# A transformer stack on one core: weights' slots and all later tiles placed 32 bytes further on

## The chip, the cores and the metric

The kernel runs on one core of a Trainium2 chip. The metric is the device time of one execution in microseconds, from the first to the last instruction. Lower is better.

## What is computed

Four layers work on 256 latent tokens and 256 context tokens of width 1024. Each layer has a token mixer of its own kind (grouped-query attention, differential attention, gated linear attention, neighbourhood attention) and then a gated MLP with a width-3 convolution. Every half is followed by a layer norm, and scales and shifts come from a modulation vector.

```python
def conv_ffn(h, w_up, conv_w, conv_b, w_down):
    u = dwconv_centred(h @ w_up, conv_w, conv_b)
    gate, val = jnp.split(u, 2, axis=-1)
    return (jax.nn.silu(gate) * val) @ w_down
...
for i in range(DEPTH):
    h = x * (1.0 + scale) + shift            # for latents and for context
    x = layer_norm(alpha * x + gate * mixer(h), ln1_g[i], ln1_b[i])
    h = x * (1.0 + scale2) + shift2
    x = layer_norm(alpha * x + gate2 * conv_ffn(h, ...), ln2_g[i], ln2_b[i])
```

In the last layer only the 256 latents go through the output projection and the MLP.

## The kernel before

Activations lie with the feature on the partition and the token in the free dimension: 128 partitions, 8 blocks of features, 512 tokens (columns 0 to 255 context, 256 to 511 latents). Every large projection is done with split numbers. A float32 value x is written as x_hi (rounded to the type fp32r) plus x_lo (the rest). `three` (L1649, the matmul itself on L1652) then issues three matmuls for each block of 128 input features: weights hi by activations hi, weights hi by activations lo, weights lo by activations hi. One of the two operands is stationary (128 columns are loaded into the array, LDWEIGHTS) and the other moves through it (256 or 512 columns). The load for the next matmul runs while the present one moves.

Weights come in slabs of 128 partitions x 1024 float32 (512 KB), by DMAs that the SP queue issues. There are four slots (`SLOTS`). Each has a raw tile `slab_raw`, a rounded one `slab_hi` that ScalarE writes (L571), and a rest `slab_lo` that VectorE writes (L1015). One output tile takes one slab and 24 matmuls. Loads and splits run three slabs ahead (`AHEAD`).

`place` (in `build_program`) hands out positions in a partition one after the other, each rounded up to 64 bytes: first `xn`, then the rounded activations `h_hi` and `h_lo` (16384 bytes each), then the four `slab_raw`, four `slab_hi` and four `slab_lo` (4096 bytes each), then the constants `cst`, the tables, the work tiles of the layer norm and the MLP, and last the tiles of each stage, which share one stretch. The MLP's second product reads `g_hi` and `g_lo`, which lie in that last stretch. `out_z` and `out_gb` of the end lie over `h_hi` and `h_lo`.

The stages of a layer follow each other: projections to q, k, v (`project`, `four_ahead`, and `v_wide` or `v_project`, where the activations are stationary and the slab moves), the mixer, the output projection, the MLP's first product (44 slabs, with `h_hi` and `h_lo` moving), its second product (24 slabs, with `g_hi` and `g_lo` moving). In layers 0 to 2 the MLP's products move 512 columns, in layer 3 they move 256. During the MLP of layers 0 to 2 VectorE also sums the next layer's modulation weights (L1040), and a group of eight short matmuls (L1726) takes these sums up now and then. The layer with gated linear attention also has one small projection whose weights `z_hi` and `z_lo` (64 columns) lie in the last stretch.

Of the kernel before, what the change touches and what calls it, by code (L numbers as in the profile page):

```python
# [47 lines left out]
PARTS_AHEAD = 2  # L48
PART_BUFS = 3
PLANES = 6  # L50
C_HV = C_VAL // C_HEADS
def constants():
    k = np.zeros((P, K_N), np.float32)
    i = np.arange(P)
    k[:, K_ID:K_ID + P] = np.eye(P)
    k[i ^ 32, K_SWAP + i] = 1.0
    k[:, K_ONES:K_ONES + P] = 1.0
    k[:, K_MEAN:K_MEAN + P] = 1.0 / D
    k[:, K_HEAD:K_HEAD + P] = (i[:, None] // HD == i[None, :] // HD)
    t = np.arange(LAT)  # L60
    nf = HD // 4
    inv = (np.float32(1.0) / np.float32(10000.0) ** (np.arange(nf, dtype=np.float32) / np.float32(nf))).astype(np.float32)
    ang = np.concatenate([(t // GRID_W).astype(np.float32)[:, None] * inv,
                          (t % GRID_W).astype(np.float32)[:, None] * inv], -1).astype(np.float32)
    pair = i % 32
    k[:, K_COS:K_COS + LAT] = np.cos(ang).T[pair]
    k[:, K_SIN:K_SIN + LAT] = np.sin(ang).T[pair] * np.where(i % HD < 32, -1.0, 1.0)[:, None]
    k[:, K_EPS], k[:, K_EPS + 1], k[:, K_EPS + 2] = NORM_EPS, LN_EPS, 1.0
    k[[C_RANK, 32 + C_RANK], K_EPS + 3] = 1.0
    for j in range(P // TILE):  # L70
        for r in range(2 * GROUPS):
            k[TILE * j + r, K_SEL + r] = 1.0
    cq = np.arange(GRID_W)
    c0 = np.clip(cq - WIN_C // 2, 0, GRID_W - WIN_C)
    col_in = (cq[None, :] >= c0[:, None]) & (cq[None, :] < c0[:, None] + WIN_C)
    window = np.tile(np.where(col_in, 0.0, -1e30).astype(np.float32)[::-1], (2, 1))
    return k, window
# [126 lines left out]
def build_program(nc, a, layers=DEPTH, probe=None):  # L204
# [7 lines left out]
    with ctx:  # L212
        top = [(nc.sbuf_base + 63) // 64 * 64]
        def place(name, shape, dt=f32, at=None):
            size = int(np.prod(shape[1:])) * mybir.dt.size(dt)
            offset = top[0] if at is None else at[0]
            (top if at is None else at)[0] += (size + 63) // 64 * 64
            return nc.alloc_sbuf_tensor_at(name, list(shape), dt, offset=offset)
        xn = place("xn", [P, DT, T])
        h_at = [top[0]]  # L220
        h_hi, h_lo = place("h_hi", [P, DT, T], f32r), place("h_lo", [P, DT, T], f32r)
        raw = [place(f"slab_raw{s}", [P, SLAB]) for s in range(SLOTS)]
        whi = [place(f"slab_hi{s}", [P, SLAB], f32r) for s in range(SLOTS)]
        wlo = [place(f"slab_lo{s}", [P, SLAB], f32r) for s in range(SLOTS)]
# [29 lines left out]
        q_dec = [place(f"q_dec{s}", [P, 2, 2 * CH], at=gla_at if s == 0 else prm_at) for s in range(2)]  # L254
        masked = [place(f"masked{p}", [P, PLANES, TILE], at=gla_at) for p in range(2)]
        scores = [place(f"scores{p}", [P, CH], at=gla_at) for p in range(2)]
# [38 lines left out]
        past_end = place("past_end", [P, 2, CH], at=at)  # L295
        near_mask = place("near_mask", [P, PLANES, TILE], at=at)
        k_endT = place("k_endT", [P, 6, C_KEY], at=at)
# [5 lines left out]
        decay = [place(f"decay{s}", [P, 2, 2, 2 * CH], at=at) for s in range(PART_BUFS)]  # L303
        state = [[place(f"state{d}{s}", [P, C_HV], at=at if s < 2 else mean_at) for s in range(3)] for d in range(2)]
        z_raw = place("z_raw", [P, DT, 64], at=z_at)
# [154 lines left out]
        def exponent_bank(*use):  # L460
            if use[0] == "part" and use[1] < PARTS_AHEAD:
                return bank[4 + 2 * use[1] + use[2]]
            return bank[7] if use == ("squares", C_HEADS - 1) else bank[exponent_uses.index(use) % 3]
# [8 lines left out]
        def near_bank(p):  # L472
            return bank[6][:, PLANES * TILE * p:PLANES * TILE * (p + 1)]
        def ends_in(g):
            return ((0,), (1, 2), (3, 4), (5,))[g]
# [81 lines left out]
        def _(act):  # L557
# [135 lines left out]
            def root(dst, of, scale):  # L693
                step.up(nc.scalar.activation(dst, of, ACT.Ln, scale=scale, bias=eps_norm))
                act.wait_ge(s_act, step.n)
                return nc.scalar.activation(dst, dst, ACT.Exp, scale=-0.5)
# [143 lines left out]
            def gla_tables():  # L840
# [13 lines left out]
                for dst, c0, n in ((summed_raw, 0, n_sums), (past_end, n_sums, n_end),  # L854
                                   (near_mask, n_sums + n_end, PLANES * TILE),
                                   (diagonal, n_sums + n_end + PLANES * TILE, P)):
                    act.dma_start(dst[:], a["k_blocks"][:, c0:c0 + n]).then_inc(S["tables_in"], 16)
# [35 lines left out]
            def gla(n_v):  # L893
# [16 lines left out]
                def head_root(hd):  # L910
                    act.wait_ge(S["ss_full"], hd + 1)
                    root(rstd[:], exponent_bank("squares", hd)[:], 1.0 / C_HV).then_inc(S["rs_ready"], 1)
                def head_hi(hd):
                    for v in range(2):
                        act.wait_ge(S["o_normed"], 2 * hd + v + 1)
                        nc.scalar.activation(h_hi[:, 2 * hd + v, :], o_head[v][:], ACT.Copy).then_inc(S["o_hi"], 1)
# [84 lines left out]
        def _(dve):  # L1001
# [382 lines left out]
            def gla(n_v):  # L1384
                S = att[2]
                def mask_near(u):
                    dve.wait_ge(S["score_full"], C_PARTS * u + C_PARTS)
                    for p in range(2):
                        if u:
                            dve.wait_ge(S["reduced"], 2 * (u - 1) + p + 1)  # L1390
                        nc.vector.tensor_tensor(masked[p][:], near_bank(p).rearrange("p (l i) -> p l i", l=PLANES),
                                                near_mask[:], ALU.mult).then_inc(S["masked"], 1)
# [20 lines left out]
                def first_states(hd):  # L1413
                    for d, slot in ((FWD, 0), (BWD, 1)):
                        dve.wait_ge(S["update_full"], 6 * hd + 2)
                        nc.vector.tensor_copy(state[d][0][:], bank[7][:, C_HV * slot:C_HV * slot + C_HV]
                                              ).then_inc(S["state"], 1)
                def next_states(hd, n):
                    for d, slot in ((FWD, 0), (BWD, 1)):
# [4 lines left out]
                        nc.vector.scalar_tensor_tensor(state[d][n][:], state[d][n - 1][:], edge[(n + 1) % 2][:, d, p:p + 1],  # L1424
                                                       bank[7][:, C_HV * slot:C_HV * slot + C_HV], ALU.mult, ALU.add
                                                       ).then_inc(S["state"], 1)
# [220 lines left out]
        def _(pe):  # L1647
# [390 lines left out]
            def gla():  # L2038
# [26 lines left out]
                def update(hd, n):  # L2065
                    pe.wait_ge(S["state"], 6 * hd + 2 * n)
                    for d, slot in ((FWD, 0), (BWD, 1)):
                        chunk = 2 * (n == 2) + int((n == 1) ^ (d == BWD))
                        pe.wait_ge(S["k_end"], end_of[chunk, d] + 1)
                        mm(bank[7][:, C_HV * slot:C_HV * slot + C_HV], k_endT[:, end_of[chunk, d], CH * hd:CH * hd + CH],  # L2070
                           v_tok[:, chunk, C_HV * hd:C_HV * hd + C_HV], start=True, stop=True).then_inc(S["update_full"], 1)
                def output(u, p):
                    hd, half, tokens = unit_of(u)
                    cs = slice(tokens.start + CH * p, tokens.start + CH * p + CH)
                    vals = v_tok[:, 2 * half + p, C_HV * hd:C_HV * hd + C_HV]
                    first = half == 0 and p == 0
                    carried = [(FWD, 2 * half + p - 1), (BWD, 2 * half - p)]
                    carried = [(d, n) for d, n in carried if n >= 0]
                    pe.wait_ge(S["scores"], 2 * u + p + 1)
                    pe.wait_ge(S["q_dec"], u + 1)  # L2080
                    if first and hd:
                        pe.wait_ge(S["squared"], 2 * hd)
                        pe.wait_ge(S["o_gated"], 2 * hd)
                    pe.wait_ge(S["state"], 6 * hd + max(2 * n + 1 + (d == BWD) for d, n in carried))
                    for v in range(2):
                        vc = slice(CH * v, CH * v + CH)
                        last = half == 1 and p == 1
                        mm(bank[4 + v][:, cs], vals[:, vc], scores[p][:], start=first, stop=False, skip_group_check=True)
                        for d, n in carried:
                            ins = mm(bank[4 + v][:, cs], state[d][n][:, vc], q_dec[u % 2][:, d, CH * p:CH * p + CH], start=False,  # L2090
                                     stop=last and (d, n) == carried[-1], skip_group_check=True)
                    ins.then_inc(S["o_full"], 1)
# [185 lines left out]
```

## Time and profile before

| | |
|---|---|
| time, median of 3 runs | 2459.04 us (2454.8 to 2460.25) |
| the profiled execution, from first to last instruction | 2459.1 us |
| its span on the page | 2459.1 us |
| matmuls | 13806, of them 10254 on L1652 |
| mean granted TensorE clock | 0.982 |

The rows below come from one profiled execution. In a timeline the first column is the start in microseconds, the second how long the instruction or the merged group took, and "x" is the count. The time between the starts of two matmuls that follow each other is what a matmul costs the engine. Its own duration is longer, since matmuls overlap. Tiles stand as out<-in, without buffer numbers.

### The profile page before, as it was taken

How to read it: one execution, taken by the hardware profiler on the slowest of the kernel's cores; microseconds unless marked ns; L12 is line 12 of the kernel's file. 1: busy time of each engine (PE TensorE's matmuls, PEld its weight loads, DVE VectorE, ACT ScalarE, POOL GpSimd, SP SyncE). 2: the span in 40 equal slices, each digit the busy share in tenths (PEclk: the TensorE clock that was granted, in tenths of full speed). 3: DMA queues.
4: the chain of work that ended last, by engine and by line, in shares of the span. 5: the costliest groups of instructions: out<-in, count | busy, mean ns of one | idle time of the engine just before them, and what ended most of it. 6: DMA issues, size and time to landing. Idle time of an engine off the chain costs nothing.

```text
span 2459.1 us, 35614 instructions
## 1 busy us (share of the span) xinstructions
PE 2342.6 (95%) x13806; PEld 1911.9 (78%) x13806; DVE 1694.4 (69%) x2573; ACT 1132.1 (46%) x1948; POOL 334.6 (14%) x266
## 2 busy tenths in 40 slices
PE   5999999999999999999999998899999999978998
PEld 3765788888888558888878777778888888847998
DVE  2376689987444776999865236768999834486874
ACT  3466554432332666443324444455343325386663
POOL 0000411111100003111112003332111011002110
PEclk8999999999999999999999999999999999999999
DMA  8621645556233022555552420044555636403664
GB/s 255 200 69 58 192 138 163 163 150 203 79 91 94 27 79 78 165 162 158 172 168 72 120 77 27 2 138 119 159 159 161 201 92 122 145 10 112 182 183 132
DMA packets 458426, 312.26 MB, mean 127 GB/s; under 512 B 24258, under 2 KB 413810, under 8 KB 458004
## 3 DMA queue, kind: packets, MB, share of 16 engines
q1 hardware_dynamic: 455488, 308.44, 42.8%
q8 instruction: 110, 1.80, 0.3%
q10 hardware_dynamic: 2772, 1.56, 0.2%
q14 instruction: 56, 0.46, 0.1%
HBM read 308.92 MB, written 1.05 MB: 126 GB/s over the span
## 4 chain that ended last, share of the span: by engine, by line
PE 83%; DVE 7%; ACT 4%; DMA 3%; issue 2%; SPq 1%; DVEq 0%; ACTq 0%
PE bank L1652 72%; PE bank L1945 2%; PE bank L1895 2%; DMA slab_raw<-in_mod_w 1%; PE bank L1915 1%; DVE stat L1281 1%; DVE slab_lo L1015 1%; ACT p L767 1%; ACT hb L586 1%; DMA slab_raw<-in_a_w_o 1%; DVE q_part L1340 1%; PE bank L1726 1%; ACT slab_hi L571 1%; SPq L536 1%; ACT pt L779 1%
## 5 line engine op out<-in xcount | busy, mean ns | idle before, releaser
L1652 PE MATMUL bank<-h_hi,slab_hi 128*128 128x512 f32 (+1 forms) x2416 | 844.3, 349 | 25.5 <-DVE slab_lo L1015 17.9
L1652 PE MATMUL bank<-h_lo,slab_hi 128*128 128x512 f32 (+1 forms) x2416 | 833.9, 345 | 0.0
L1652 PE MATMUL bank<-h_hi,slab_lo 128*128 128x512 f32 (+1 forms) x2416 | 833.6, 345 | 0.0
L1015 DVE TENSOR_TENSOR slab_lo<-slab_raw,slab_hi 128x1024 fp32r<-128x1024 f32 (+1 forms) x388 | 522.7, 1348 | 309.8 <-ACT slab_hi L571 308.6
L571 ACT ACTIVATE slab_hi<-slab_raw 128x1024 fp32r<-128x1024 f32 (+1 forms) x388 | 400.7, 1034 | 313.7 <-PE bank L1652 228.4
L1652 PEld LDWEIGHTS bank<-h_hi,slab_hi 128*128 128x128 f32 x2416 | 463.5, 192 | 102.9 <-issue 42.6
L1652 PEld LDWEIGHTS bank<-h_lo,slab_hi 128*128 128x128 f32 x2416 | 463.9, 192 | 53.2 <-issue 0.5
L1652 PEld LDWEIGHTS bank<-h_hi,slab_lo 128*128 128x128 f32 x2416 | 463.4, 192 | 53.7
L989 ACT ACTIVATE conv<-bank,prm 128x512 f32<-128x512 f32 (+1 forms) x176 | 127.7, 726 | 447.4 <-PE bank L1652 447.3
L1040 DVE SCALAR_TENSOR_TENSOR mod_sum<-slab_raw,cond_wide,mod_sum 128x512 f32<-128x512 f32 x420 | 317.6, 814 | 0.3 <-DMA slab_raw<-in_mod_w 0.3
L1652 PE MATMUL bank<-g_hi,slab_hi 128*128 128x512 f32 (+1 forms) x770 | 268.3, 348 | 2.1 <-ACT res_t L623 2.1
L1652 PE MATMUL bank<-g_hi,slab_lo 128*128 128x512 f32 (+1 forms) x770 | 267.2, 347 | 0.0
L1652 PE MATMUL bank<-g_lo,slab_hi 128*128 128x512 f32 (+1 forms) x770 | 266.3, 346 | 0.0
L1643 POOL TENSOR_TENSOR g<-conv,conv 128x512 f32<-128x512 f32 (+1 forms) x88 | 126.0, 1431 | 728.2 <-DVE conv L1552 728.2
L1652 PEld LDWEIGHTS bank<-g_hi,slab_hi 128*128 128x128 f32 x770 | 144.6, 188 | 26.4 <-issue 5.0
L1549 DVE SCALAR_TENSOR_TENSOR conv<-bank,prm,conv 128x510 f32<-128x510 f32 (+1 forms) x176 | 118.9, 676 | 63.7 <-ACT conv L989 62.3
L1652 PEld LDWEIGHTS bank<-g_lo,slab_hi 128*128 128x128 f32 x770 | 144.4, 188 | 19.5
L1652 PEld LDWEIGHTS bank<-g_hi,slab_lo 128*128 128x128 f32 x770 | 144.7, 188 | 18.6
L1100 DVE SCALAR_TENSOR_TENSOR xn<-xn,coef,res_t 128x256 f32<-128x256 f32 (+1 forms) x79 | 47.0, 595 | 117.4 <-ACT res_t L623 117.4
L1587 POOL TENSOR_TENSOR acc_s<-acc_s,xn 128x256 f32<-128x256 f32 (+1 forms) x57 | 72.0, 1263 | 389.8 <-DVE xn L1100 389.8
L1552 DVE SCALAR_TENSOR_TENSOR conv<-bank,prm,conv 128x510 f32<-128x510 f32 (+1 forms) x176 | 120.1, 682 | 6.2
L623 ACT ACTIVATE res_t<-bank,coef,modT 128x256 f32<-128x256 f32 x112 | 59.4, 560 | 128.4 <-PE bank L1652 128.4
(242 smaller groups left out, 2657.6 us busy)
## 6 DMA issues: line engine op xcount, KB each, us to landing
slab_raw<-in_ffn_w_up SPq DMA_DIRECT2D x176, 512.0 KB, 3.9
slab_raw<-in_mod_w SPq DMA_DIRECT2D x168, 512.0 KB, 4.6
slab_raw<-in_ffn_w_down SPq DMA_DIRECT2D x64, 512.0 KB, 3.7
slab_gap<-in_mod_w SPq DMA_DIRECT2D x24, 512.0 KB, 7.9
slab_raw<-in_ffn_w_down SPq DMA_DIRECT2D x32, 384.0 KB, 3.2
slab_raw<-in_b_w_qkv SPq DMA_DIRECT2D x24, 512.0 KB, 3.7
slab_raw<-in_c_w_in SPq DMA_DIRECT2D x24, 512.0 KB, 3.8
slab_raw<-in_d_w_qkv SPq DMA_DIRECT2D x24, 512.0 KB, 4.1
```

The costliest lines, as they stand in the source:

```text
L571: nc.scalar.activation(whi[slot][:, 0:w], raw[of][:, 0:w], ACT.Copy).then_inc(s_hi, 1)
L623: ins = nc.scalar.activation(res_t[e % 2][:, cc], bank[(fg + ev.dt) % 4][:, cc], ACT.Identity, bias=coef[st % 2][:, 5, ev.dt:ev.dt + 1], s ...
L989: nc.scalar.activation(conv[k][u][:, c], bank[(fg + 2 * j + k) % 4][:, c], ACT.Identity, bias=prm[:, R_LAYER * i + R_CB + tile:R_LAYER * i ...
L1015: nc.vector.tensor_tensor(wlo[slot][:, 0:w], raw[of][:, 0:w], whi[slot][:, 0:w].bitcast(f32), ALU.subtract).then_inc(s_lo, 1)
L1040: ins = nc.vector.scalar_tensor_tensor(to[:, s, :], part, factor, to[:, s, :], ALU.mult, ALU.add)
L1549: nc.vector.scalar_tensor_tensor(dst[:, :, 1:LAT], ps[:, :, 0:LAT - 1], prm[:, w:w + 1], dst[:, :, 1:LAT], ALU.mult, ALU.add).then_inc(s_t ...
L1552: nc.vector.scalar_tensor_tensor(dst[:, :, 0:LAT - 1], ps[:, :, 1:LAT], prm[:, 4 * FT + w:4 * FT + w + 1], dst[:, :, 0:LAT - 1], ALU.mult, ...
L1587: nc.gpsimd.tensor_tensor(acc_s[:, ev.cols], acc_s[:, ev.cols], xn[:, ev.dt, ev.cols], ALU.add).then_inc(s_sum, 1)
L1643: nc.gpsimd.tensor_tensor(g32[u][:, c], conv[0][u][:, c], conv[1][u][:, c], ALU.mult).then_inc(s_gmul, 1)
L1652: ins = mm(out, l, r, start=first and n == 0, stop=last and n == 2)
L1895: mm(b[:, 0:nk], qk[r, qt, q0:q0 + P], keys, start=True, stop=True).then_inc(S["score_full"], 1)
L1945: ins = mm(bank[6 + o % 2][HD * odd:HD * odd + HD, CTX * s:CTX * s + 256], v_tok[:, kt, HD * vh:HD * vh + HD], pt[2 * (quad % 2) + odd][:, ...
```

## The change

After `h_lo` the next free position moves on by 32 bytes more. `slab_raw`, `slab_hi`, `slab_lo` and every tile that is placed behind them then start 32 bytes later in each partition. `xn`, `h_hi` and `h_lo` stay where they are, and so do `out_z` and `out_gb`, which lie over them. No instruction is added, removed or moved, and no size changes.

```diff
@@ -48,6 +48,7 @@
 PARTS_AHEAD = 2
 PART_BUFS = 3
 PLANES = 6
+H_GAP = 32
 C_HV = C_VAL // C_HEADS
 def constants():
     k = np.zeros((P, K_N), np.float32)
@@ -219,6 +220,7 @@
         xn = place("xn", [P, DT, T])
         h_at = [top[0]]
         h_hi, h_lo = place("h_hi", [P, DT, T], f32r), place("h_lo", [P, DT, T], f32r)
+        top[0] += H_GAP
         raw = [place(f"slab_raw{s}", [P, SLAB]) for s in range(SLOTS)]
         whi = [place(f"slab_hi{s}", [P, SLAB], f32r) for s in range(SLOTS)]
         wlo = [place(f"slab_lo{s}", [P, SLAB], f32r) for s in range(SLOTS)]
```

## Rows read from the trace of the kernel before

**Rows 1.** The page, busy time of each engine (us, share of the span, instructions).

```profile
PE 2342.6 (95%) x13806; PEld 1911.9 (78%) x13806; DVE 1694.4 (69%) x2573; ACT 1132.1 (46%) x1948; POOL 334.6 (14%) x266
```

**Rows 2.** The page, the chain that ended last: by engine, by line.

```profile
PE 83%; DVE 7%; ACT 4%; DMA 3%; issue 2%; SPq 1%; DVEq 0%; ACTq 0%
PE bank L1652 72%; PE bank L1945 2%; PE bank L1895 2%; DMA slab_raw<-in_mod_w 1%; PE bank L1915 1%; DVE stat L1281 1%; DVE slab_lo L1015 1%; ACT p L767 1%; ACT hb L586 1%; DMA slab_raw<-in_a_w_o 1%; DVE q_part L1340 1%; PE bank L1726 1%; ACT slab_hi L571 1%; SPq L536 1%; ACT pt L779 1%
```

**Rows 3.** TensorE's matmuls grouped by line and shape: count, busy us, mean ns.

```profile
L1652 PE MATMUL bank<-h_hi,slab_hi 128*128 128x512 f32 x1360 | 536.7, 395 | 6.0 <-DVE slab_lo L1015 5.5 <-ACT scores L900 0.5
...
L1652 PE MATMUL bank<-h_hi,slab_hi 128*128 128x256 f32 x1056 | 307.6, 291 | 19.5 <-DVE slab_lo L1015 12.4 <-DVE h_lo L1080 7.1
...
L1652 PE MATMUL bank<-g_hi,slab_lo 128*128 128x512 f32 x462 | 181.5, 393 | 0.0
...
L1652 PE MATMUL bank<-g_hi,slab_hi 128*128 128x256 f32 x308 | 86.9, 282 | 2.1 <-ACT res_t L623 2.1
...
L1652 PE MATMUL bank<-slab_hi,h_hi 128*128 128x512 f32 x192 | 78.8, 410 | 0.8 <-DVE v_tok L1205 0.8
...
L1652 PE MATMUL bank<-slab_hi,h_hi 128*128 128x256 f32 x32 | 9.8, 307 | 0.0
```

**Rows 4.** The chain in order of time, in the MLP's first product, layer 1.

```profile
1059.05 60.07 PE bank L1652 x264
1119.12 1.00 PE bank L1726 x8
1120.12 60.07 PE bank L1652 x264
```

**Rows 5.** Timeline of TensorE, same stage, first and seventh of seven matmuls.

```profile
1099.92 0.39 PE L1652 MATMUL bank<-h_hi,slab_hi 128*128 128x512 f32 x1
...
1101.28 0.39 PE L1652 MATMUL bank<-h_hi,slab_hi 128*128 128x512 f32 x1
```

**Rows 6.** Timeline, MLP's first product of layer 3, first and tenth of ten matmuls.

```profile
2299.75 0.28 PE L1652 MATMUL bank<-h_hi,slab_hi 128*128 128x256 f32 x1
...
2300.83 0.28 PE L1652 MATMUL bank<-h_hi,slab_hi 128*128 128x256 f32 x1
```

**Rows 7.** Timeline, MLP's second product, context columns, first and thirteenth of thirteen matmuls.

```profile
1312.78 0.28 PE L1652 MATMUL bank<-g_hi,slab_hi 128*128 128x256 f32 x1
...
1314.14 0.28 PE L1652 MATMUL bank<-g_hi,slab_hi 128*128 128x256 f32 x1
```

**Rows 8.** Timeline, MLP's second product, latent columns, first and eleventh of eleven matmuls.

```profile
2409.75 0.28 PE L1652 MATMUL bank<-g_hi,slab_hi 128*128 128x256 f32 x1
...
2410.93 0.28 PE L1652 MATMUL bank<-g_lo,slab_hi 128*128 128x256 f32 x1
```

**Rows 9.** Timeline, MLP's second product, 512 columns, first and eighth of eight matmuls.

```profile
1224.77 0.39 PE L1652 MATMUL bank<-g_hi,slab_lo 128*128 128x512 f32 x1
...
1226.38 0.39 PE L1652 MATMUL bank<-g_hi,slab_hi 128*128 128x512 f32 x1
```

**Rows 10.** Timeline, the projection with 64 stationary columns, first and eleventh of eleven matmuls.

```profile
1389.06 0.39 PE L1652 MATMUL bank<-h_hi,z_hi 128*64 128x512 f32 x1
...
1391.39 0.39 PE L1652 MATMUL bank<-h_lo,z_hi 128*64 128x512 f32 x1
```

**Rows 11.** Windows, MLP's first product of layer 1, of layer 3: length, PE, PEld, DVE, ACT, POOL busy.

```profile
981.60:1202.80 221.20, 221.20 (x987) 180.41 (x986) 207.13 (x256) 91.49 (x122) 33.58 (x21) 1.00 0.54 162
2242.80:2382.00 139.20, 130.97 (x1071) 130.09 (x1071) 112.53 (x163) 88.83 (x147) 23.60 (x26) 0.98 0.58 166
```

**Rows 12.** VectorE's groups by line and shape, the convolution's two side taps.

```profile
L1552 DVE SCALAR_TENSOR_TENSOR conv<-bank,prm,conv 128x510 f32<-128x510 f32 x132 | 98.8, 749 | 4.7
L1549 DVE SCALAR_TENSOR_TENSOR conv<-bank,prm,conv 128x510 f32<-128x510 f32 x132 | 97.9, 742 | 49.2 <-ACT conv L989 47.9
```

**Rows 13.** The page, DMA: the weights' queue, and one group of issues (KB, us to landing).

```profile
q1 hardware_dynamic: 455488, 308.44, 42.8%
slab_raw<-in_ffn_w_up SPq DMA_DIRECT2D x176, 512.0 KB, 3.9
```

## The prediction

> **What bounds the kernel now.** I read the page's busy times first. TensorE is busy for 95% of the span, VectorE for 69%, and nothing else for more than half, weight loads apart [rows 1]. Then I read the chain that ended last: 83% of it is TensorE, and 72% is the one line L1652, the split projections [rows 2]. A piece of that chain shows how tightly these stages run: 264 matmuls in 60.07 us, a short group of 1.00 us, and 264 more in 60.07 us [rows 4]. With 0.39 us for the last matmul that is (60.07 - 0.39) / 263 = 0.2269 us from start to start. No other engine appears between them, so the cost of one matmul times their number sets the time there. The question is then only whether the distance between two matmuls depends on where their operands lie.
>
> For that I read the distances themselves. In the MLP's first product six steps take 1.36 us, 226.7 ns each, for 512 columns [rows 5]. With 256 columns nine steps take 1.08 us, 120.0 ns each [rows 6]. The difference is 106.7 ns for 256 columns, 0.417 ns a column, which at the granted clock of 1.00 [rows 11] is one column in each cycle of 2.4 GHz. So 512 columns are 213.3 ns and 256 are 106.7 ns, and both kinds pay the same 13.3 ns on top. I call this the extra.
>
> The same instruction with other tiles has another extra. With `g` moving, the context columns take 1.36 us for twelve steps, 113.3 ns each, an extra of 6.7 [rows 7]. The latent columns take 1.18 us for ten, 118 ns, an extra of 11 [rows 8]. With 512 columns of `g` it is 1.61 us for seven, 230 ns, an extra of 17 [rows 9]. With the stationary tile `z`, which has only 64 columns to load, ten steps take 2.33 us, 233 ns, an extra of 20 although less is loaded [rows 10]. All of these run at the same types and mostly the same shapes. What differs is position. By the sizes in `place`, the weights' slots lie whole multiples of 4096 bytes behind `h_hi`, so both operands start at the same place within any 128 bytes. `g_hi`, `g_lo`, `z_hi` and `z_lo` lie 64 bytes off that. I can't exclude another reason (the engines around it, the place in PSUM), since no row has the same stage at two positions.
>
> **The change, part by part.** It removes and adds no instruction. It moves four things.
>
> The pair of weights' slot and `h`. Before, the two operands of these matmuls are 0 bytes apart within 128, after it 32 bytes. The counts are 3 x 1360 with 512 columns and 3 x 1056 with 256, and with the slab moving 3 x 192 and 3 x 32 [rows 3]. That is 4656 of the wide kind and 3264 of the narrow, 7920 in all. At 226.7 and 120.0 ns they are 1055 + 392 = 1447 us, 59% of the span.
>
> No row shows a distance of 32 bytes, so I bound it. Below: the extra can't go under nothing, so 7920 x 13.3 ns = 105 us is the most there is to win. Above: the worst extra in the rows is `z`'s 20, which is 6.7 more, and 7920 x 6.7 = 53 us lost. For the narrow kind the best row is 113.3 ns, which is 6.7 less: 3264 x 6.7 = 21.8 us. For the wide kind every row at another distance is above 226.7, but a narrow matmul loads the same 128 columns of weights, and there the extra fell. I take a third of the narrow kind's gain, 2.2 ns: 4656 x 2.2 = 10.3 us. Together 32 us.
>
> Not all of it lies on the path. L1652 has 72% of the chain, 1771 us [rows 2]. All its matmuls by their distances are 1447 us, plus 1386 with 512 columns of `g` at 230 (319 us) and 924 with 256 at 118 (109 us), 1875 us in all [rows 3, 8, 9]. So 94% is on the path and 32 us become 30 us.
>
> What covers the rest would have to follow. In layer 1's first product VectorE is busy for 207 of 221 us [rows 11]. It becomes the bound there once TensorE is over 6% faster, that is under 212 ns a matmul, which is less than the columns alone. So VectorE does not cap the 2.2 ns, nor 6.7. In layer 3's it has 112.5 of 139, and the narrow matmuls would have to fall under 97 ns [rows 11].
>
> The pair of weights' slot and `g` moves as a whole, and so do transposes against `cst`: distance kept, own position 32 bytes on. I count 0. The bounds are the same 6.7 ns either way on 2310 matmuls, 15 us, if each operand's own position is what matters and not the distance.
>
> VectorE, ScalarE and GpSimd read and write most tiles 32 bytes on. The convolution's left tap writes from the second element of its tile on, 4 bytes in, and reads from the first. The right tap does it the other way round. They take 742 and 749 ns [rows 12]. An offset that is no multiple of 64 costs at most 1% here, on engines that have slack. I count 0. If it cost 1% on VectorE's 7% share of the chain [rows 2] it would be 2 us.
>
> The DMAs write slabs 32 bytes on, as 512-byte pieces. The queue is busy for 42.8% and a slab lands 3.9 us after its issue, with three slabs of 24 matmuls ahead of it [rows 13]. Only the 3% of the chain that are DMA would feel it, 74 us [rows 2]. If a piece took 5% more that is 4 us; I count 0.
>
> The sum is 2459 - 30 = 2429 us. The profiled execution is 2459.1 us and the median of the runs 2459.04, so no correction is needed.
>
> **A rule against it.** The row: seven thousand matmuls pay 13.3 ns that the columns don't explain, and others pay 6.7 [rows 6, 7]. The Trainium skill, SBUF — State Buffer, section "Who interferes with whom", gives TensorE two read ports, one for each operand, and says that "PE and ACT never wait on anyone". By it the distance between the operands can't matter and the change would do nothing. The same page, section "Door 1", counts SBUF lines of 16 bytes, and 32 bytes are two whole lines, so by that too nothing changes. This case's rows don't bear the first out, since distances differ at one shape.
>
> **The rivals.**
>
> *Nothing happens.* The extra belongs to the stage and not to the position: for instance to what is written in PSUM, or the order of stationary and moving tiles. For it: the extra of 13.3 ns is the same in all stages with `h`, whichever slot is read and also with the slab moving. Against it: `g` and `h` go through the same code with 24 matmuls a tile. Time 2459. The rule above gives the same.
>
> *The distance of 32 is worse than 0.* For it: two of the three other kinds of row at 512 columns are above 226.7, by 3 (`g`) and by 6 (`z`) [rows 9, 10], and 512 columns are 73% of the time in question. Against it: both 256-column rows are below 120. Its mechanism is that loads and moving reads meet more often. With the wide kind 3 to 6 ns up and the narrow unchanged it costs 14 to 28 us, x 0.94 = 13 to 26, so 2472 to 2485; with both at `z`'s extra 50 us, 2509. It decides where the wide kind's rise is over 0.7 of the narrow kind's fall (3264 / 4656).
>
> *The whole extra shrinks.* Both kinds fall by the 6.7 of the best row: 53 us x 0.94 = 50, so 2409. At the bound of no extra at all, 99 us, so 2360. Against it: no row with 512 columns is under 226.7.
>
> *The loads pay.* DMAs into slots 32 bytes off take longer, and stages that wait for weights grow: 4 us for 5%, 2463. It decides if landing takes more than three slabs' matmuls.
>
> **How the numbers follow.** Chances: narrow kind falls and the wide one a little, 0.30 (2429, own range 2415 to 2445); whole extra shrinks, 0.15; nothing, 0.25; distance worse, 0.26; loads pay, 0.04. From no change a measurement of this kernel can tell 0.2%, 5 us. Faster 0.45, same 0.26 with the smallest part of the last rival, slower 0.29. The range goes from 2395, beyond 2409 and short of the bound, to 2488, just above the 2485 of the worse distance. It leaves out the deeper half of the third rival and the `z` case for both kinds, under 0.2 together.
>
> **What would show it.** In the timeline of the changed kernel, ten matmuls with 256 columns of `h` in 1.02 us instead of 1.08, and seven with 512 in 1.35 instead of 1.36; the chain's pieces of 264 matmuls in 59.5 us instead of 60.07. The distances with `g` unchanged. The mean durations of rows 12 and the landing of rows 13 unchanged. The prediction is wrong if the distances with `h` are the same to the nanosecond, or if the wide kind rises, or if any time comes from elsewhere than L1652.

## The result

The change makes the kernel slower: 2481.72 us median (2478.38 to 2487.3, 4 runs) against 2456.92 us (2452.56 to 2460.25, 4 runs). The ratio is 1.0105, with a 95% interval of 1.0087 to 1.0122, so about 25 us more. The prediction was 2429 us with a range of 2395 to 2488. The time lies in the range but on the other side of no change, and the likeliest case was wrong. The time of the rival "the distance of 32 is worse than 0", 2472 to 2485, is what came.

The page of the changed kernel shows the same work: the same instruction counts, and the same engine bounds it. These are its busy times and, in the next line, the DMA queue of the weights (compare [rows 1, 13]).

```profile
PE 2361.2 (95%) x13806; PEld 1902.5 (77%) x13806; DVE 1696.2 (68%) x2573; ACT 1132.0 (46%) x1948; POOL 335.8 (14%) x266
...
q1 hardware_dynamic: 455488, 308.44, 42.5%
...
slab_raw<-in_ffn_w_up SPq DMA_DIRECT2D x176, 512.0 KB, 3.9
```

VectorE, ScalarE and GpSimd are busy as long as before to about 2 us, and a slab lands after the same 3.9 us. TensorE alone is busy for longer, by 19 us. The chain in order of time shows it in the MLP's first product of layer 1 (the line of `three` is L1654 now, and the short group is L1728):

```profile
1066.54 61.80 PE bank L1654 x264
1128.34 0.99 PE bank L1728 x8
1129.33 61.80 PE bank L1654 x264
```

Before, the same 264 matmuls took 60.07 us [rows 4]. That is 1.73 us more, 6.6 ns a matmul. The timeline of TensorE at the same place:

```profile
1099.24 0.40 PE L1654 MATMUL bank<-h_hi,slab_lo 128*128 128x512 f32 x1
...
1101.57 0.40 PE L1654 MATMUL bank<-h_hi,slab_hi 128*128 128x512 f32 x1
```

Ten steps in 2.33 us are 233 ns, where it was 226.7 [rows 5]. With 256 columns the step went the other way. In layer 3's first product thirteen steps take 1.54 us, 118.5 ns, where it was 120.0 [rows 6]:

```profile
2299.78 0.28 PE L1654 MATMUL bank<-h_lo,slab_hi 128*128 128x256 f32 x1
...
2301.32 0.28 PE L1654 MATMUL bank<-h_hi,slab_lo 128*128 128x256 f32 x1
```

Of `g`, which keeps its distance from the slots, the latents' 256 columns are as before (14 steps in 1.65 us, 118 ns [rows 8]). With 512 columns most slabs are as before, and the first 7 of 20 in each of the layers 0 to 2 went up to 232 to 233 ns (last two rows below, 7 steps in 1.63 us, where it was 1.61 [rows 9]). The small projection with `z` went down, 11 steps in 2.51 us, 228 ns instead of 233 [rows 10]:

```profile
2409.32 0.28 PE L1654 MATMUL bank<-g_hi,slab_hi 128*128 128x256 f32 x1
...
2410.97 0.28 PE L1654 MATMUL bank<-g_hi,slab_lo 128*128 128x256 f32 x1
...
1402.73 0.40 PE L1654 MATMUL bank<-h_hi,z_hi 128*64 128x512 f32 x1
...
1405.24 0.39 PE L1654 MATMUL bank<-h_hi,z_lo 128*64 128x512 f32 x1
...
1224.83 0.40 PE L1654 MATMUL bank<-g_hi,slab_lo 128*128 128x512 f32 x1
...
1226.46 0.40 PE L1654 MATMUL bank<-g_hi,slab_hi 128*128 128x512 f32 x1
```

For the sum I took the start times of all of L1652's matmuls in both traces (whole nanoseconds, mean over the steps inside each slab). With 512 columns of `h`, or of a slab against stationary `h`: 227.05 before, 233.3 after, 4656 x 6.25 = 29.1 us more. With 256: 119.95 before, 118.3 after, 3264 x 1.65 = 5.4 us less. With 512 columns of `g`: 228.96 and 230.5, 1386 x 1.57 = 2.2 us more. With 256 of `g` no change. Together 25.9 us, and with the 94% on the path 24 us. The medians differ by 24.8. The two profiled executions differ by less, 2459.1 and 2476.3 us. Matched matmul by matmul, the time between two neighbours on this line grew by 23.1 us in all, and the rest became 5.8 us shorter. That rest was also 3 to 7 us shorter in the profiled executions of all the whole kernels below, so it tells of the one profiled execution of the kernel before and not of the change. Single executions of one kernel spread by 8 us.

### The profile page after: what moved, and what is told of

Read it like the earlier page. It is cut to its first block, busy times and chain, and to the rows that moved or that the text cites. A ratio compares the mean times of both kernels' runs of the same rounds, so it can differ in the third digit from the quotient of the medians.

```text
span 2476.3 us, 35614 instructions
## 1 busy us (share of the span) xinstructions
PE 2361.2 (95%) x13806; PEld 1902.5 (77%) x13806; DVE 1696.2 (68%) x2573; ACT 1132.0 (46%) x1948; POOL 335.8 (14%) x266
## 4 chain that ended last, share of the span: by engine, by line
PE 83%; DVE 7%; ACT 4%; DMA 3%; issue 2%; SPq 1%; ACTq 0%; POOL 0%; DVEq 0%; POOLq 0%
PE bank L1654 73%; PE bank L1947 2%; PE bank L1897 1%; DMA slab_raw<-in_mod_w 1%; PE bank L1917 1%; DVE stat L1283 1%; DVE slab_lo L1017 1%; ACT p L769 1%; DMA slab_raw<-in_a_w_o 1%; ACT hb L588 1%; PE bank L1709 1%; PE bank L1728 1%; ACT slab_hi L573 1%; ACT pt L781 1%; DMA slab_raw<-in_d_w_qkv 1%
## 5 line engine op out<-in xcount | busy, mean ns | idle before, releaser
L1654 PE MATMUL bank<-h_hi,slab_hi 128*128 128x512 f32 (+1 forms) x2416 | 848.9, 351 | 26.6 <-DVE slab_lo L1017 19.0
L1654 PE MATMUL bank<-h_lo,slab_hi 128*128 128x512 f32 (+1 forms) x2416 | 839.1, 347 | 0.0
L1654 PE MATMUL bank<-h_hi,slab_lo 128*128 128x512 f32 (+1 forms) x2416 | 838.8, 347 | 0.0
L1654 PEld LDWEIGHTS bank<-h_hi,slab_hi 128*128 128x128 f32 x2416 | 458.8, 190 | 111.9 <-issue 43.2
L1654 PEld LDWEIGHTS bank<-h_hi,slab_lo 128*128 128x128 f32 x2416 | 459.1, 190 | 62.0
L1654 PEld LDWEIGHTS bank<-h_lo,slab_hi 128*128 128x128 f32 x2416 | 459.2, 190 | 61.0 <-issue 0.5
L1654 PE MATMUL bank<-g_hi,slab_hi 128*128 128x512 f32 (+1 forms) x770 | 269.6, 350 | 2.1 <-ACT res_t L625 2.1
L1654 PE MATMUL bank<-g_lo,slab_hi 128*128 128x512 f32 (+1 forms) x770 | 267.8, 348 | 0.0
L1654 PE MATMUL bank<-g_hi,slab_lo 128*128 128x512 f32 (+1 forms) x770 | 267.2, 347 | 0.0
L1654 PEld LDWEIGHTS bank<-g_hi,slab_hi 128*128 128x128 f32 x770 | 144.8, 188 | 27.5 <-issue 5.0
L1654 PEld LDWEIGHTS bank<-g_hi,slab_lo 128*128 128x128 f32 x770 | 144.8, 188 | 19.5
L1654 PEld LDWEIGHTS bank<-g_lo,slab_hi 128*128 128x128 f32 x770 | 144.7, 188 | 19.0
```

Source lines behind the costliest of these rows:

```text
L1654: ins = mm(out, l, r, start=first and n == 0, stop=last and n == 2)
```

## The experiments

Three theories stood against each other after the result. Theory A: what counts is the distance between the positions of the two operands, within some power of two. Theory B: each operand's own position counts. Theory C: other engines' accesses to moved tiles slow TensorE's reads. In what follows the distance is the position of the stationary operand minus that of the moving one, within 256 bytes. The kernel before was timed again beside the experiments: 2454.6 us (11 executions) and, for the layouts at the end, 2454.57 us (23).

### The distances in isolation

A kernel without the network: TensorE issues the three products of `three`, 48 matmuls for each pair of tiles, on tiles placed at chosen positions (`K` is 4). The output is a copy of an input. `PAIRS` holds the stationary tile at 14 distances from the moving one, then both moved, then repeats. It was executed once.

```python
W_AT = (0, 4, 16, 32, 48, 64, 80, 96, 112, 128, 160, 192, 224, 256)
...
            for cols in (512, 256):
                for xa, wa in PAIRS:
                    for rep in range(4):
...
                        for k in range(K):
...
                            for n, s in enumerate((0, 1, 0)):
                                ins = nc.tensor.matmul(out[:, 0:cols], w[wa][:, wc], x[xa][s][:, xc],
...
```

> This kernel leaves the network out: TensorE alone issues split-style fp32r matmuls, 48 for each pair of a stationary and a moving tile, first with 512 and then with 256 columns, the tiles placed 0 to 256 bytes off a multiple of 4096; the output is a copy of an input. Theory A (the distance between the two operands' positions within some power of two sets the extra): distance 0 gives 226.7 and 120.0 ns, distance 32 gives 233.3 and 118.3, distance 64 about 229 and 113 to 118, with both operands shifted by 32 or 64 as with both at 0, and the pattern comes back at 128 or at 256. Theory B (each operand's own position): both shifted by 32 differs from both at 0. Theory C (neither; what the other engines and DMAs do to the reads): all pairs the same, near the columns' 213.3 and 106.7 ns.

The timeline, only rows of `x_lo` (each third matmul). With 512 columns the first two rows are distance 256 (21 steps, 4.76 us, 226.7 ns), the next two distance 32 (21 steps, 4.90 us, 233.3 ns), the next two both operands moved by 32 (21 steps, 4.77 us, 227 ns), the last two distance 192, which is -64 (21 steps, 4.81 us, 229 ns).

```profile
176.06 0.39 PE L51 MATMUL bank<-x_lo,w 128*128 128x512 f32 x1
...
180.82 0.39 PE L51 MATMUL bank<-x_lo,w 128*128 128x512 f32 x1
...
64.48 0.40 PE L51 MATMUL bank<-x_lo,w 128*128 128x512 f32 x1
...
69.38 0.40 PE L51 MATMUL bank<-x_lo,w 128*128 128x512 f32 x1
...
186.97 0.39 PE L51 MATMUL bank<-x_lo,w 128*128 128x512 f32 x1
...
191.74 0.39 PE L51 MATMUL bank<-x_lo,w 128*128 128x512 f32 x1
...
153.93 0.39 PE L51 MATMUL bank<-x_lo,w 128*128 128x512 f32 x1
...
158.74 0.39 PE L51 MATMUL bank<-x_lo,w 128*128 128x512 f32 x1
```

All distances, from the start times, mean of the second half of each 48:

| distance | 512 columns, ns | 256 columns, ns |
|---|---|---|
| 0 (also both operands at 32, both at 64, and 256) | 226.7 | 120.0 |
| 4 | 232.3 | 118.2 |
| 16 | 233.4 | 118.4 |
| 32 | 233.4 | 118.4 |
| 48 | 233.3 | 117.7 |
| 64 (repeated later) | 233.2 (233.4) | 113.4 (117.7) |
| 80 | 232.0 | 118.7 |
| 96 (repeated later) | 234.3 (234.6) | 118.9 (117.4) |
| 112 | 233.4 | 119.8 |
| 128 | 233.5 | 118.9 |
| 160 | 233.4 | 120.0 |
| 192 (-64; the other pair with -64) | 228.8 (229.0) | 117.8 (113.4) |
| 224 (-32; the other pair with -32) | 233.3 (233.3) | 117.9 (116.7) |

Nothing but TensorE runs while these matmuls do, and the kernel's steps come out to the nanosecond: 226.7 and 120.0 at distance 0, 233.4 and 118.4 at 32. That ends theory C for these steps. Both operands moved together give what both at 0 give, which ends theory B. One expectation fell: 229 ns with 512 columns came at -64, and +64 took 233. The pattern does not come back at 128 but at 256. For 512 columns distance 0 is the best place, -64 costs 2 ns more, and even 4 bytes cost most of the full price. For 256 columns it is the worst place or nearly so. At 64 bytes either way two values occur, 113.4 and 117.7. The pair (0, +64) gave both, 113.4 the first time and 117.7 when it was repeated on the same tiles, so position alone does not pick the value.

### Activations moved too

```diff
+        top[0] += 32
         h_at = [top[0]]
         h_hi, h_lo = place("h_hi", [P, DT, T], f32r), place("h_lo", [P, DT, T], f32r)
```

> The 32 bytes are put ahead of the rounded activations, so activations, slots and all later tiles move together. Theory A (distance): 226.7 and 120.0 ns are back and the time is that of the kernel before, 2457 us. Theory B (position of the weights or of the later tiles): slower as the changed kernel, about 2480 us.

2457.83 us against 2454.6, a ratio of 1.0017 (1.0007 to 1.0028). All slots, tables and work tiles start where they do in the changed kernel, and nearly the whole loss is gone. The chain's piece is that of the kernel before to 0.01 us:

```profile
1056.60 60.07 PE bank L1653 x264
```

A rest of 3 us, just outside no change by its interval, doesn't come from L1653, whose steps are those of before to 0.01 ns in the mean. I did not find where it is. The slabs with 512 columns of `g` take 228.8 to 229.5 ns here but for the last of each layer (227.5), although `g` and slots lie at the very positions of the changed kernel, where the first 7 of 20 took 232 to 233. So their two values do not come from position either.

### Only the tiles behind the slots

```diff
         wlo = [place(f"slab_lo{s}", [P, SLAB], f32r) for s in range(SLOTS)]
+        top[0] += 32
         cst = place("cst", [P, K_N])
```

> The 32 bytes are put behind the slots, so only constants, tables and work tiles move, slots and h stay. Theory A: the matmuls with h stay at 226.7 and 120.0 ns; those with g are now 96 bytes off within 128 and may change by up to 6.7 ns each on 2310, 15 us; time 2457 plus or minus 15. Theory C (slower reads and writes of the other engines on tiles 32 bytes off): about 2480 us.

2465.06 us against 2454.6, 1.0051 (1.0036 to 1.0066). The matmuls with `h` keep their 226.7 and 120.0 ns. Those with `g` are now at distance 160 and take 233.4 ns with 512 columns (eight steps in 1.87 us below) and 120.0 with 256:

```profile
1249.77 0.39 PE L1653 MATMUL bank<-g_lo,slab_hi 128*128 128x512 f32 x1
...
1251.64 0.39 PE L1653 MATMUL bank<-g_hi,slab_hi 128*128 128x512 f32 x1
```

1386 x 4.4 + 924 x 3.2 ns = 9.1 us, against 10.5 measured. The isolated table has 233.4 and 120.0 for distance 160. So most of the loss here is in TensorE's steps again. The 1.4 us that are left, up to about 7 by the interval, are for everything else, the other engines' work on tiles 32 bytes off included.

### Slots 64 bytes on

```diff
         h_hi, h_lo = place("h_hi", [P, DT, T], f32r), place("h_lo", [P, DT, T], f32r)
+        unit_gb = place("unit_gb", [P, 2, DT])
...
-        unit_gb = place("unit_gb", [P, 2, DT])
```

> The 64-byte table unit_gb is placed ahead of the slots, so slots lie 64 bytes off h and later tiles stay. Theory A with a period of 128 bytes: h gets what g had, about 229 ns for 512 columns and 113.3 to 118 for 256, and g gets 226.7 and 120.0; 4656 times 2.2 up and 3264 times 2.2 to 6.7 down gives minus 11 to plus 3 us, and g takes back about 1 us. With a period of 64 bytes: no change at all. Theory B: the weights' own position makes h and g change alike.

The tables between the slots and the old place of `unit_gb` move by 64 bytes as well. 2470.41 us against 2454.6, 1.0073 (1.0057 to 1.009). Half of the expectation fell. `g` got 226.7 and 120.0 as expected, but `h` with 512 columns did not get `g`'s 229. It takes 233.3 ns (eight steps in 1.87 us), and the slabs that move against stationary `h`, at distance -64, take about 229. With 256 columns `h` has two values that hold for rows of 24 matmuls: of 130 rows 71 take 117.8 ns, all of layer 3 from the output projection on among them (below, twelve steps in 1.41 us), and 50 take 113.3.

```profile
1099.74 0.40 PE L1652 MATMUL bank<-h_hi,slab_hi 128*128 128x512 f32 x1
...
1101.61 0.40 PE L1652 MATMUL bank<-h_hi,slab_lo 128*128 128x512 f32 x1
...
2299.75 0.28 PE L1652 MATMUL bank<-h_hi,slab_hi 128*128 128x256 f32 x1
...
2301.16 0.28 PE L1652 MATMUL bank<-h_hi,slab_hi 128*128 128x256 f32 x1
```

So the sign of the distance matters with 512 columns: +64 took 233.3 in every row there is, here and in the isolated table, and -64 took 229 in all but the 21 slabs of `g` in the changed kernel. The period of 128 that I had assumed was wrong. In the kernel before, `g` stands at -64 and `z` at +64, which fits that `z` had the larger extra [rows 9, 10]. The table does not carry over to 64 stationary columns, though: `z` takes 227.9 ns at distance 96 in the changed kernel, where 128 stationary columns take 234.3.

### Column counts, and which load counts

The isolated kernel again, executed once, with other column counts, alternating positions, and one moving tile for all three products.

```python
SIZES = [(c, 1, (d,), (0,)) for c in (512, 384, 256, 192, 128) for d in (0, 32, 64, 128, 192)]
OWN_OR_NEXT = [(512, 1, (0,), (0,)), (512, 1, (0, 32), (0, 32)), (512, 1, (0, 32), (32, 0)), (512, 1, (0,), (0,)),
               (256, 1, (0,), (0,)), (256, 1, (0, 64), (0, 64)), (256, 1, (0, 64), (64, 0)), (256, 1, (0,), (0,))]
```

> TensorE alone again, no network, 48 matmuls for each case; the output is a copy of an input. Distance means stationary position minus moving position within 256 bytes. Three questions. (1) Columns 512, 384, 256, 192 and 128 at distances 0, 32, 64, 128, 192: if the loss comes only while 128 weights load beside the moving reads, the extra at 512 and at 384 is the same (13.3 ns at distance 0, 20 at 32), and at 192 and 128 the load sets the step, near 107 ns plus something. (2) Positions that alternate: if what counts is the load of the NEXT stationary tile against the present moving one, then stationary 0, 32, 0, 32 with moving 32, 0, 32, 0 gives 226.7 ns although each matmul's own pair is 32 apart, and stationary and moving both 0, 32, 0, 32 gives 233 ns although its own pair is 0 apart. If the matmul's own pair counts, it is the other way round. (3) One moving tile for all three products, not hi and lo: no difference to the split pattern.

Steps in ns, mean of the last 24 of each 48:

| distance | 512 | 384 | 256 | 192 | 128 columns |
|---|---|---|---|---|---|
| 0 | 226.7 | 173.3 | 120.0 | 111.7 | 111.7 |
| 32 | 233.3 | 173.3 | 118.3 | 111.7 | 111.7 |
| 64 | 233.3 | 174.5 | 117.8 | 111.7 | 111.7 |
| 128 | 232.7 | 176.0 | 118.5 | 111.7 | 111.7 |
| 192 | 228.9 | 173.3 | 117.8 | 111.7 | 111.7 |

With 192 and 128 columns the step is 111.7 ns at every distance. It no longer falls with the columns, so something else sets it, and position is free. That this is the load of the 128 weights is likely but not shown. Between 256 and 512 columns the price of distance 32 turns from -1.7 over 0 to +6.7 ns. The extra at a distance is therefore not one fixed amount for one load, as I had expected of this run. With one moving tile for all products nothing changes (226.7 and 233.3).

The alternating cases decide nothing cleanly. With 512 columns, own pair 0 apart and the next load 32 off gives 231.7 ns. Own pair 32 apart and the next load at 0 gives 230.0 ns, which is neither 226.7 nor 233.3. Both are between the pure cases. With 256 columns and 64 bytes the same two cases gave 116.7 and 120.0 ns. The second is the value of distance 0 and the first lies between the two values of 64, as if the next load counted. Which of the two loads meets the moving reads stays open.

### Layouts that use it

`g` 192 bytes further, so that its distance is 0 (a few tiles behind it, such as `hb`, move along):

```diff
+G_SHIFT = 192
...
-        at = [arena]
+        at = [arena + G_SHIFT]
         g_hi, g_lo = place("g_hi", [P, FT, T], f32r, at=at), place("g_lo", [P, FT, T], f32r, at=at)
```

> The old layout with g alone 192 bytes further, so distance 0 for g. 512 columns of g 229.0 to 227.0 ns, 2.7 us less; 924 with 256 columns from 116.8 to 119.9 ns, 2.9 us more: no change, 2455.

2455.43 us against 2454.57, 1.0002 (0.9992 to 1.0012). That is as expected: 229.0 to 226.8 ns with 512 columns, 116.8 to 119.9 with 256, and the two cancel.

The next two add that in layer 3, where only the latents are left and all matmuls from the output projection on have 256 columns, `h` and `g` are written and read some columns further down in their tiles, in columns that the context no longer uses. Nothing else is moved, and the columns written in PSUM stay.

```diff
+        def back_of(c, narrow):
+            return slice(c.start - BACK, c.stop - BACK) if narrow else c
...
-                    ins = three(out[:, c], whi[slot][:, wc], wlo[slot][:, wc], x_hi[:, k0 + k, c], x_lo[:, k0 + k, c],
+                    ins = three(out[:, c], whi[slot][:, wc], wlo[slot][:, wc], x_hi[:, k0 + k, xc], x_lo[:, k0 + k, xc],
```

With `BACK` 48, a distance of -64:

> The old layout, but g lies 192 bytes further (distance 0 within 256 instead of -64), and in layer 3 the latents' activations and g stand 48 columns further down in their tiles, so distance -64 for all 256-column matmuls from the output projection on. Distance theory: 1386 matmuls with 512 columns of g fall from 229.0 to 227.0 ns (2.7 us), 396 with 256 rise from about 116 to 120 (1.6 us, behind the context and latent halves), layer 3's 1248 with h fall from 120.0 to 117.8 or 113.3 (2.7 to 8.4 us), its 528 with g stay at 117.8 or fall to 113.3 (0 to 2.4 us). Sum 4 to 12 us faster, 2443 to 2451 against 2455. If layout has nothing more to give: 2455.

2451.19 us against 2454.57, 0.9987 (0.9977 to 0.9997): 3.4 us faster, just short of the 4 to 12 expected. Layer 3's steps are 113.3 ns in the output projection and 117.8 in both products of the MLP.

With `BACK` 16, a distance of +64:

> As b1, with 16 columns instead of 48, so distance +64 for the 256-column matmuls of layer 3. The isolated loop had 113.6 and 117.8 ns there, and the kernel with slots 64 bytes on had both: 4 to 12 us faster, 2443 to 2451.

2443.51 us against 2454.57, 0.9953 (0.9941 to 0.9966), 11.1 us faster and at the upper end of what was expected. Here all of layer 3's steps from the output projection on are 113.3 ns, for `h` and for `g`. The chain has 1566 matmuls of layer 3's MLP in one piece, of the kernel before first, then with 48, then with 16:

```profile
2253.96 188.46 PE bank L1652 x1566
```

```profile
2243.53 187.11 PE bank L1659 x1566
```

```profile
2245.94 180.18 PE bank L1659 x1566
```

The timeline of the kernel with 16 (thirteen steps in 1.47 us, 113 ns):

```profile
2299.82 0.28 PE L1659 MATMUL bank<-h_hi,slab_hi 128*128 128x256 f32 x1
...
2301.29 0.28 PE L1659 MATMUL bank<-h_lo,slab_hi 128*128 128x256 f32 x1
```

This one is faster than both kernels: by 0.5% than the one before, and by about 1.5% than the changed one (1.0105 / 0.9953, each against the kernel before). The distance alone did not earn it. The kernel with slots 64 bytes on has +64 in layer 3 too, and there all these matmuls of `h` took 117.8 ns. Which of the two values a layout gets is not predicted by anything here.

## Why the prediction was wrong

**The bound.** Right. L1652's steps times their counts set the time. 24 us worked out from the steps stand against 24.8 measured, which fits the share of 94% on the path.

**The mechanism.** Right as far as it went: the extra of a split matmul depends on the position of its operands. The isolated loop, and the kernel in which `h` moves too, show that it is their distance.

**The step that failed** is the term for the wide kind: "a narrow matmul loads the same 128 columns of weights, and there the extra fell. I take a third of the narrow kind's gain, 2.2 ns: 4656 x 2.2 = 10.3 us." It measured 6.25 ns the other way, 29 us lost. All the rows of the wide kind at another distance were above 226.7 [rows 9, 10], and I set the one argument from the narrow kind over them. The worst row's 20 ns of extra was the right figure for this distance: 233.3 - 213.3 = 20.0. That was partly luck, since this row, `z`, stands at another distance and loads 64 columns.

**The narrow kind.** Right in sign, too large in size: 1.65 ns in place of 6.7, 5.4 us in place of 21.8. 113.3 ns belongs to a distance of 64 bytes either way and not to every distance but 0.

**The distance "within 128".** Wrong. The pattern comes back at 256 bytes and not at 128, and with 512 columns the sign matters, so `g` and `z`, which I took for the same case, were not.

**`g` counted at 0.** Nearly right: 2.2 us inside the 15 I had bounded. It is one of two values for a whole slab, 228.9 or 233.3, and a third of them got the worse one. Position did not pick it, as the kernel with `h` moved too shows. What did is not shown.

**VectorE, ScalarE, DMA at 0.** Right. The taps take 749 and 743 ns, before 749 and 742 [rows 12], and a slab lands after 3.9 us. The working for VectorE was weaker than it looked: both taps have an operand 4 bytes off, so comparing them could not bound what such a place costs. That 32 more bytes changed neither does.

```profile
L1554 DVE SCALAR_TENSOR_TENSOR conv<-bank,prm,conv 128x510 f32<-128x510 f32 x132 | 98.9, 749 | 4.7
L1551 DVE SCALAR_TENSOR_TENSOR conv<-bank,prm,conv 128x510 f32<-128x510 f32 x132 | 98.1, 743 | 63.6 <-ACT conv L991 63.5
```

**The rival that decided.** Its point of turning, a rise of the wide kind over 0.7 of the narrow kind's fall, was met (6.25 against 1.65), and its 13 to 26 us held 24.8. Its mechanism, loads and moving reads that meet more often, is not shown by any run.

**The rule of the Trainium skill** (SBUF — State Buffer, "Who interferes with whom") gives TensorE two independent read ports, and the prediction drew from it that distance can't matter. It does: 226.7 and 233.4 ns are the same matmuls, on the same engine alone, with one operand 32 bytes on. Whether a port waits there isn't shown. The lines of 16 bytes, which the prediction took from "Door 1" of that page, leave nothing unchanged either: 16 bytes cost 6.7 ns, as much as 32.

What stays open is the mechanism inside the chip: why the price depends on the distance within 256 bytes, why it changes sign between 512 and 256 columns, and what picks one of the two values at 64 bytes.

## What to carry to other kernels

Where a stage is a dense row of fp32r matmuls, read the step between their starts and compare stages of the same shape: a difference of some nanoseconds can come from where stationary and moving tile lie, and times some thousand matmuls it is a per cent. The figures that follow are for 128 stationary columns. With 512 moving columns keep the two at the same place within 256 bytes. With 256 columns try 64 bytes apart, and measure it, since two values occur there, 113.3 and 117.8 ns against 120.0. When a term of the sum has rows of its own kind, take those, even if another kind has a more welcome number.

## What the hardware showed that I had not expected

- The distance counts within 256 bytes, and 4 bytes off are nearly as dear as 32 (232.3 and 233.4 ns against 226.7).
- At 384 columns distances 0 and 32 cost the same, 173.3 ns.
- At 192 and 128 columns the step is 111.7 ns at every distance tried.
- Two values for the same distance and the same positions, held over whole slabs: 113.3 or 117.8 ns at 64 bytes with 256 columns, 228.9 or 233.3 at -64 with 512.
